# Two transitions between matrix stages of a two-block network: row-panel order, updates in pieces and a pre-norm scale applied after the products

## The reference

```
# block 1 (h is meta + x, 272 rows; the meta rows are dropped at the end)
u = rms_norm(h, norm_mix_pre)
u = conv mixer(u): (u @ w_in) -> a * sigmoid(g) -> causal depthwise conv, 31 taps
                   -> layer_norm -> silu -> @ conv_w_out + b_out
h = h + rms_norm(u, norm_mix_post)                              # first transition
u = (silu(n @ w_gate) * (n @ w_up)) @ w_down,  n = rms_norm(h, norm_ffn_pre)
h = h + rms_norm(u, norm_ffn_post)                              # second transition
# block 2
proj = rms_norm(h, norm_mix_g_2) @ w_in_2      -> b, c, hc, z, gate logits
y    = short conv(b, c, hc) @ w_up_conv, spatial gating(gelu(z)) @ w_up_sgu
h = h + (sig(g1)*y1 + sig(g2)*y2) @ w_out_2                     # third transition
n = rms_norm(h, norm_ffn_g_2); router picks 1 of 4 groups and 2 of its 4 experts
h = h + sum over chosen experts of gate * ((silu(n@wg) * (n@wu)) @ wd)
out = rms_norm(h, norm_final_g_2)
rms_norm(x, g) = x * rsqrt(mean(x*x) + 1e-6) * g
```

## Time and profile before

| | |
|---|---|
| timed runs | 2414.32 us median (2413.07 to 2415.45) |
| profiled execution | 2415.2 us, span 2413.2 us |
| TensorE busy | 2320.2 us (96%) |
| VectorE, ScalarE, GpSimd busy | 1599.2 (66%), 1273.8 (53%), 174.2 us (7%) |
| mean granted clock of TensorE | 0.974 |
| DMA | 510.87 MB, mean 212 GB/s |

### The profile page before, as it was taken

One profiled execution on the slowest core, in us unless ns is written; L12 is line 12 of the kernel. 1 busy time (PEld: TensorE's weight loads), 2 busy tenths in 40 slices (PEclk: granted clock), 3 DMA queues, 4 the chain that ended last, 5 costly groups with the idle time before them and its releaser, 6 DMA issues.

```text
span 2413.2 us, 34884 instructions
## 1 busy us (share of the span) xinstructions
PE 2320.2 (96%) x12133; PEld 1976.1 (82%) x12133; DVE 1599.2 (66%) x1785; ACT 1273.8 (53%) x1243; POOL 174.2 (7%) x67
## 2 busy tenths in 40 slices
PE   9999897999999999997999999999979999999997
PEld 8999686888888878886888888887767777777775
DVE  3999666555555554446576654575568888888887
ACT  4444446555555544445443544443346776766775
POOL 4676000000000000000020000000000000000000
PEclk8999898999999999998999999999979999999998
DMA  7555155666766745555576676654529989899894
GB/s 199 167 156 168 70 194 154 188 187 181 192 191 187 193 159 191 192 192 183 146 202 184 172 192 191 180 177 171 187 79 341 348 315 365 318 347 339 316 365 187
DMA packets 494081, 510.87 MB, mean 212 GB/s; under 512 B 12204, under 2 KB 407108, under 8 KB 475076
## 3 DMA queue, kind: packets, MB, share of 16 engines
q1 hardware_dynamic: 492660, 504.30, 65.6%
q0 software_dynamic: 1104, 5.78, 0.7%
q10 hardware_dynamic: 272, 0.20, 0.0%
HBM read 508.15 MB, written 2.10 MB: 211 GB/s over the span
## 4 chain that ended last, share of the span: by engine, by line
PE 85%; DVE 6%; ACT 4%; DMA 2%; issue 2%; ACTq 0%; DVEq 0%; SPq 0%
PE ps L1785 23%; PE ps L1725 17%; PE ps L1790 12%; PE ps L1918 7%; PE ps L1934 6%; PE ps L1922 4%; ACT whi L522 3%; PE ps L1635 3%; PE ps L1636 2%; PE ps L1658 2%; DVE wlo L926 2%; PE ps L1820 2%; DMA raw<-in_w_exp_up 1%; PE ps L1899 1%; DMA raw<-in_w_exp_gate 1%
## 5 line engine op out<-in xcount | busy, mean ns | idle before, releaser
L926 DVE TENSOR_TENSOR wlo<-raw,whi 128x2048 fp32r<-128x2048 f32 x444 | 1017.3, 2292 | 338.7 <-ACT whi L522 337.2
L522 ACT ACTIVATE whi<-raw 128x2048 fp32r<-128x2048 f32 x476 | 911.6, 1916 | 535.1 <-PE ps L1725 220.1
L1785 PE MATMUL ps<-xT,whi 128*128 128x512 f32 x2688 | 647.6, 392 | 7.3 <-DVE xT L1278 4.2
L1785 PEld LDWEIGHTS ps<-xT,whi 128*128 128x128 f32 x2688 | 494.8, 189 | 103.5 <-issue 4.4
L1790 PEld LDWEIGHTS ps<-xT,wlo 128*128 128x128 f32 x2688 | 347.1, 191 | 15.7 <-DVE wlo L926 1.3
L1790 PE MATMUL ps<-xT,wlo 128*128 128x256 f32 x2688 | 351.6, 283 | 0.9 <-DVE wlo L926 0.9
L1725 PE MATMUL ps<-whi,act 128*128 128x512 f32 x1168 | 282.5, 395 | 3.2 <-ACT act L619 3.2
L1725 PEld LDWEIGHTS ps<-whi,act 128*128 128x128 f32 x1168 | 223.0, 191 | 52.4 <-ACT act L619 3.7
L1918 PE MATMUL ps<-whi,moe_r 128*128 128x512 f32 x1024 | 258.3, 394 | 6.1 <-ACT whi L522 6.1
L694 ACT ACTIVATE wk<-ps 128x256 f32<-128x256 f32 x184 | 68.8, 384 | 353.0 <-PE ps L1790 352.7
L1918 PEld LDWEIGHTS ps<-whi,moe_r 128*128 128x128 f32 x1024 | 191.5, 189 | 49.5 <-ACT whi L522 7.6
(11 more groups left out here) (263 smaller groups left out, 1748.3 us busy)
## 6 DMA issues: line engine op xcount, KB each, us to landing
raw<-in_w_in SPq DMA_DIRECT2D x72, 1024.0 KB, 5.5
raw<-in_w_exp_gate SPq DMA_DIRECT2D x64, 1024.0 KB, 5.4
raw<-in_w_exp_up SPq DMA_DIRECT2D x64, 1024.0 KB, 5.7
raw<-in_w_exp_down SPq DMA_DIRECT2D x64, 1024.0 KB, 5.9
raw<-in_ffn_w_gate SPq DMA_DIRECT2D x44, 1024.0 KB, 5.6
raw<-in_ffn_w_up SPq DMA_DIRECT2D x44, 1024.0 KB, 5.6
raw<-in_ffn_w_down SPq DMA_DIRECT2D x44, 1024.0 KB, 4.8
raw<-in_conv_w_in SPq DMA_DIRECT2D x32, 1024.0 KB, 6.0
```

Of the source, the lines that this page charges most:

```text
L522: fn(whi[:, s % 2, :], raw[:, s % RING, :], ACT.Copy).then_inc(hi_ready, 1)
L926: V.tensor_tensor(wlo[:, s % 2, :], raw[:, s % RING, :], whi[:, s % 2, :], ALU.subtract).then_inc(lo_ready, 1)
L1785: mm(ps[:, bank, :], whi[:, s % 2, at:at + P], xT5[:, k0 + k, :], start=(k == 0), stop=False)
```

## The change

- **Last two row panels** (`last_row_pair` for `last_row_panel`, three stages): both panels' products of token half 0 first, `tok_done` after each of its four pieces; then half 1 piece by piece, with a `tok_done` for each.
- **`post`** (ScalarE, VectorE): waits for each piece by itself; `h` is updated in 512-column pieces, each telling `add_done`. ScalarE's first high half of the next stage comes behind the squares.
- **No scale before the turn**: `pre` is gone at the first two transitions. TensorE turns the unscaled rows of `h` as an ordinary fp32 product with the identity. The squares of `h` (`row_squares`), roots and reciprocals come after the turn. The reciprocals become a 128x256 broadcast: VectorE scales the identity (`rs_d`), TensorE multiplies by `ones` (`scale_rows`), VectorE copies it (`rsB`).
- **The scale is applied later**: in the feed-forward to the gate panel after `joined` (the up panel's scale goes into the post-norm's epsilon, `BIAS2`), in ZV's gelu by per-row scalars, and in CH, BG, U, GT to every panel after `joined` (one product more on VectorE).
- **GpSimd makes the first two low halves** of C and of ZV, once all updates of `h` are done; TensorE waits for `lo_pool` there.
- At the first transition TensorE runs panels 0 and 1 of the feed-forward interleaved with the turns; at the second it turns tiles 8 to 15 between the products of ZV's first two panels.
- At the third transition, the adds wait for single pieces; `pre` stays.

```diff
# GpSimd
+            def lo(n, s, added):
+                pool.wait_ge(add_done, added)
+                pool.wait_ge(hi_ready, n + s + 1)
+                pool.tensor_tensor(wlo[:, s, :], raw[:, s, :], whi[:, s, :], ALU.subtract).then_inc(lo_pool, 1)
+            lo(C, 0, 8)
+            lo(C, 1, 8)
             pool.wait_ge(post_done, 8)
             pool.dma_start(gB[:, :], norm_ffn_post.to_broadcast([P, D])).then_inc(gain_in, 16)
+            lo(ZV, 0, 16)
+            lo(ZV, 1, 16)
...
# ScalarE
             post(0, C)
-            turn(1, V_FPRE, 0)
+            turn(1, V_FPRE, 0, C, {4: 1})          # hi(C, 1) ahead of tile 4
+            row_squares(0, 0)
+            hi(C, 2)
+            row_squares(0, 1)
+            row_roots(0)
...
+            turn(2, V_MIX2, 4, ZV, {8: 1, 12: 2})
+            row_squares(1, 0)
+            row_squares(1, 1)
+            row_roots(1)
...
# VectorE
+                def added(t):
+                    v.wait_ge(root_ready, 2 + 4 * q + t + 1)
+                    own.mark(V.reciprocal(st[:, RS + t:RS + t + 1], st[:, RT + t:RT + t + 1]))
+                    own.wait(v)
+                    v.wait_ge(post_done, 8 * q + NC * (t + 1))
+                    for c in range(NC):
+                        hc = h[:, t, c * BANK:(c + 1) * BANK]
+                        V.scalar_tensor_tensor(out=hc, in0=tmp[:, t, c * BANK:(c + 1) * BANK], scalar=st[:, RS + t:RS + t + 1],
+                                               in1=hc, op0=ALU.mult, op1=ALU.add).then_inc(add_done, 1)
+                for b in range(NC):
+                    gained(b)
+                total(q, 0)
+                gained(NC)
+                gained(NC + 1)
+                added(0)
+                total(q, 1)
+                gained(NC + 2)
+                gained(NC + 3)
+                added(1)
...
+            def joined(f, s, bank, dst, scaled=None):
                 v.wait_ge(feat_half, f + (s + 1))
-                V.tensor_tensor(dst, ps[:, bank, 0:T], t1[:, s % 2, :], ALU.add).then_inc(feat_free, 1)
+                ins = V.tensor_tensor(dst, ps[:, bank, 0:T], t1[:, s % 2, :], ALU.add)
+                if scaled is not None:
+                    own.mark(ins)
+                    own.wait(v)
+                    ins = V.tensor_tensor(dst, dst, rsB[scaled], ALU.mult)
+                ins.then_inc(feat_free, 1)
...
# TensorE
+            def last_row_pair(n, step):
+                for s in (2, 3):
+                    pe.wait_ge(hi_ready, n + (s + 1))
+                    pe.wait_ge(act_hi, step + s + 1)
+                    part(s, 0, whi, 0, range(NC))
+                    pe.wait_ge(act_lo, step + s + 1)
+                    part(s, 1, whi, 0, range(NC))
+                    pe.wait_ge(lo_ready, n + (s + 1 - B))
+                    for c in range(NC):
+                        i = part(s, 0, wlo, 0, (c,))
+                        if s == 3:
+                            i.then_inc(tok_done, 1)
+                for c in range(NC):
+                    for s in (2, 3):
+                        part(s, 0, whi, 1, (c,))
+                        part(s, 1, whi, 1, (c,))
+                        i = part(s, 0, wlo, 1, (c,))
+                        if s == 2 and c == NC - 1:
+                            i.then_inc(mm_done, 1)
+                    i.then_inc(mm_done if c == NC - 1 else tok_done, 1)
...
+            def turn_rows_of(q, i, bank, halves=range(TOK)):
+                for t in halves:
+                    pe.wait_ge(add_done, 8 * q + NC * t + (NC if t == 0 else i // 2 + 1))
+                    for k in range(2):
+                        at = (2 * i + k) * P
+                        ins = mm(ps[:, bank + i % 4, k * T + t * P:k * T + (t + 1) * P], h[:, t, at:at + P], ident[:, :], start=True, stop=True)
+                if 1 in halves:
+                    ins.then_inc(turned, 2)
...
-            turn(1, 0)
+            for i in range(4):
+                turn_rows_of(0, i, 0, (0,))
+            for i in range(4):
+                turn_rows_of(0, i, 0, (1,))
+            pe.wait_ge(feat_free, F_C + 2)
+            pe.wait_ge(hi_ready, C + 1)
+            for i in range(4, KT // 2):
+                pe.wait_ge(xlo_ready, KT + 2 * (i - 3))
+                turn_rows_of(0, i, 0)
+                hi_product(0, 2 * i - 8)
+                hi_product(0, 2 * i - 7)
+            pe.wait_ge(hi_ready, C + 2)
+            for k in range(KT // 2, KT):
+                pe.wait_ge(xlo_ready, KT + k + 1)
+                hi_product(0, k)
+                hi_product(1, k - KT // 2)
...
-            turn(2, 4)
+            pe.wait_ge(add_done, 8 + NC + 1)
+            for i in range(4):
+                turn_rows_of(1, i, 4)
             for b in range(4):
                 open_bank(b)
             for q in range(8):
+                if q == 1:
+                    late_rows(6)
+                    late_rows(7)
...
                 banks(0, whi)
                 banks(1, whi)
+                if q == 0:
+                    late_rows(4)
+                    late_rows(5)
+                if q < 2:
+                    pe.wait_ge(lo_pool, 2 * KT + 2 + q + 1)
+                else:
+                    pe.wait_ge(lo_ready, ZV + q + 1 - B)
                 banks(0, wlo).then_inc(mm_done, 1)
+                if q == 4:
+                    pe.wait_ge(xlo_ready, 3 * KT)
+                    scale_rows(2, 4)
+            pe.wait_ge(rs_copied, 1)
```

More of the change, by code:

```diff
@@ L635, in b_group @@
                 for s in range(4):
-                    if not (last and s == 3):
+                    if not (last and s >= 2):
                         hi(j + B, s + 2)
@@ L678, in pre, with turn @@
                     root(st[:, SS + t:SS + t + 1], st[:, RT + t:RT + t + 1], 1.0 / D, st[:, EPS_AT:EPS_AT + 1])
-            def turn(count, gain, bank):
+            def turn(count, gain, bank, n, panels):
                 for k in range(KT):
+                    if k in panels:
+                        hi(n, panels[k])
                     a.wait_ge(turned, KT * count + k + 1 + (k + 1) % 2)
@@ L700, in _ @@
                     half(g * 4 + F_C, s, 4 + s)
-                    hi(g * 4 + C, s + 2)
+                    if not (first and s == 0):
+                        hi(g * 4 + C, s + 2)
                     if s % 2:
@@ L1143, in _ @@
                         v.wait_ge(hid_ready, g * 2 + (s // 2 + 2))
-                    joined(g * 4 + F_C, s, 4 + s, xs[:, 2 if s % 2 else s // 2, :])
-                    lo(g * 4 + C, s + 2)
+                    joined(g * 4 + F_C, s, 4 + s, xs[:, 2 if s % 2 else s // 2, :], scaled=None if s % 2 else 0)
+                    if not (first and s < 2):
+                        lo(g * 4 + C, s + 2)
                     if s % 2:
@@ L1151, in _ @@
                         V.tensor_tensor(tile_of(tiles, g * 2, s // 2), sg[:, s // 2, :], xs[:, 2, :], ALU.mult).then_inc(hid_ready, 1)
+            c_group(0, first=True)
+            with rounds(v, FT // 2 - 1, (own, 4)) as g:
+                c_group(g + 1)
             def rows(n0, src, step, count):
@@ L1228, in _ @@
                     own.wait(v, 1)
[L1229 removed]
+                    joined(r * 4 + f, s, 4 + s, xs[:, s % 2, :], scaled=1)
                     lo(r * 4 + BG, s + 2)
@@ L1243, in _ @@
             own.wait(v)
-            with rounds(v, CT // 4, (own, 4)) as r:
+            with rounds(v, CT // 4, (own, 8)) as r:
                 for s in range(4):
@@ L1792, in feature_panel, with feature_stage @@
                 return i
-            def feature_stage(n0, f0, count, arrival=None):
-                peeled = 1 if arrival else 0
-                for s in range(4 * peeled):
-                    feature_panel(n0, s, f0 + s + 1, 4 + s, arrival=None if s else arrival).then_inc(mm_done, 1)
-                with pe.Fori(peeled, (count) // 4) as r:
+            def feature_stage(n0, f0, count, first=0):
+                for s in range(first, first and 4):
+                    feature_panel(n0, s, f0 + s + 1, 4 + s).then_inc(mm_done, 1)
+                    if s == first:
+                        scale_rows(1, 0)
+                with pe.Fori(1 if first else 0, (count) // 4) as r:
                     j = r * 4
```

203 lines of the change are left out of this document (117 added, 86 removed).

## The result

| | before | changed |
|---|---|---|
| timed runs | 2414.32 us median (2411.15 to 2417.36, 9 runs) | 2407.83 us median (2405.1 to 2413.27, 9 runs) |
| ratio | | 0.9974, 95% interval 0.9964 to 0.9984 |
| profiled execution | 2415.2 us, span 2413.2 | 2408.69 us, span 2406.9 |
| VectorE, ScalarE, GpSimd busy | 1599.2, 1273.8, 174.2 us | 1636.6, 1216.3, 190.4 us |
| mean granted clock | 0.974 | 0.979 |

The changed kernel is 6.5 us faster, 0.26%. In a second comparison, with both kernels timed beside two others, the ratio was 0.9968 (0.9956 to 0.998).

The account below looks back on a forecast made before the run. TensorE was busy nearly all the span, so only its waits and slow stretches could be won. 6.7 + 4.5 + 1.1 - 3.5 - 0.5 = 8.3 us off 2415.2 gave 2406.9 profiled, 2406 for the median; range 2399 to 2413.

Parts of the forecast that it names:

- Edit 1: Last two row panels run as a pair in three stages: TensorE stalls 0.6 us for VectorE's low half at each.
- Edits 2 and 3: First transition: updates by pieces, unscaled rows turned, panels 0 and 1 interleaved; gain 7.2 less 0.5 = 6.7 us.
- X: Forecast end of the last row product in the changed kernel: T + 0.6 us, the stall of the paired panels included.
- T: The end of TensorE's last row product ahead of a transition, from which times there are counted.
- Edit 4: Second transition: TensorE idles until X + 4.15, the clock is taken as down, then unscaled rows are turned; gain 4.5 us.
- rival A: No lock behind ZV and a clock kept through the second transition's gap: 14 us gained, 2400 us; chance 0.2.
- Edit 5: Added scale products: 3.5 us lost at the fourth CH panel behind ZV, 0.5 at the first gate panel.
- the lock: VectorE's instructions with two SBUF inputs and GpSimd's share a port pair exclusively, so they wait in turn; 3.5 us behind ZV.
- Edit 6: Third transition, updates by pieces only: turns start at T + 6.5 instead of T + 7.6; gain 1.1 us.
- B: The lock costs 5.5 us and the clock falls in the first transition: 1.3 us gained, 2413 us; chance 0.2.
- C: Fp32 identity products neither hold nor raise the clock: first transition 9.4 us later, second 4.4; 2420 us; chance 0.06.

Follow-up runs that it names:

- e6: Kernel before with only the paired last row panels, updates by pieces and the changed third transition; scale still ahead of the transposes: 2411.94 us, one run.
- e3: Changed kernel with GpSimd's low halves no longer waiting for the updates of h: 2415.5 us, one run.
- e7: Changed kernel with the first transition's two low halves made by VectorE instead of GpSimd: 2409.82 us, one run.
- e5: Changed kernel with fp32 products that lead nowhere added in the second transition's gap and ahead of the fourth CH panel: 2410.14 us, one run.
- e4: Changed kernel without the scale products behind the joins of CH, BG, U and GT: 2404.0 us, one run.
- e2: Changed kernel with the rows of h turned by TensorE transposes instead of fp32 products with the identity: 2402.21 us, one run.
- e8: Changed kernel with transposes for feature tiles 8 to 15 alone, identity products kept for tiles 0 to 7: 2408.09 us, one run.

## Why the prediction was right

The forecast was 2406.9 for the profiled execution (2408.69 came) and 2406 for the median (2407.83). By its steps:

- *Edit 1, stall of 0.6 us at each stage.* From row to row about 0.8, 0.8 and 0.7, of which 0.42 stands in the record as the wait for `wlo`. The forecast booked it in the gains of the three transitions, so I take it off the columns below. In the DN column, +1.1, the other 0.3 is the first panel at a low clock.
- *Edits 2 and 3, first transition.* Updates were to end at X + 1.65 and X + 5.8; with X = T here they end at T + 1.7 and T + 5.8. The third panel was to start at X + 22.05 and starts at T + 21.8. Predicted 7.2 less 0.5 = 6.7, measured 7.7 less 0.8 = 6.9. The forecast's 401.15 for the third panel before stands in the earlier trace rows as 401.26, and its 0.6 us for an update is 0.7 (2.74 / 4). e6 confirms that the pieces are the small part, e3 that GpSimd must stand behind the updates, e7 that its help is worth 0.25.
- *Edit 4, second transition.* Idle 3.84 (4.15 predicted), 5.47 for the products (5.7), CH at T + 57.9 (58.5). The forecast set its 1186.9 against 1191.4, but the row is at 1191.64, so by its own terms it had 4.7. Predicted 4.5, measured 5.9 less 0.8 = 5.1. The clock fell as the forecast took it to; e5 prices the fall at 1.6 us, against 2.2 in rival A.
- *Edit 5, the lock.* Predicted 3.5 + 0.5, measured by e4 3.5 + 0.5, with another 0.5 in that column that e4 has too. The make-up differed, and the equal sums are luck in part. The forecast took 3.5 us of pure wait and left the clock out. The wait was 2.85, a wait of 0.91 of the kernel before went, and the clock fell in the wait: the sixteen narrow products behind it took 3.58 us instead of 2.08. e2, e3 and e8 have the same wait (2.85 to 2.87), but the clock held and the narrow products took 2.17 to 2.18; their column is 1.4 us lower. So about 2.1 us are the lock's and 1.4 the clock's. The Trainium skill's rule of an exclusive lock for the whole instruction (SBUF — State Buffer, section SBUF: two separate sides) fits the alternation, and e3 shows a larger case of it than the forecast used: two instructions of 0.7 us each waited for one of 4.9.
- *Edit 6, third transition.* The restart wait is 5.79 (5.9 predicted), -1.7 less the stall of 0.7: 1.0 against 1.1.
- *Not foreseen:* 0.6 to 0.7 us at the up panels, where the clock was down for longer behind the gap of 4.28 us (4.18 before), and the scatter of 5 us of the conv stage's clock, as large as the gain.
- *The sum.* The foreseen terms measured 6.9 + 5.1 + 1.0 - 3.5 - 0.5 = 9.0 us, against 8.3. Behind ZV 0.5 more was lost, at the up panels 0.7, ahead of the first T and in the DN stage 0.3 each, and behind the last product 1.5; the last column gave 0.6 back. That makes the 6.3 us of the spans. The parts ahead of the first T, in the last column and behind the last product differ by 5.0, 1.8 and 1.1 us between the two profiles of the changed kernel, so the total says less for the forecast than the terms by stage do.

Of the rivals, A failed on the lock and on the clock. B's fall of the clock in the first transition did not come, and the lock with the fall behind it cost 3.5 us, not 5.5. The terms that C names for its first transition add up to about X + 29, not X + 31.5, so its 2420 should have been some 2 us less. C is refuted by the first transition, where the clock stayed at 1.00 under the products with the identity, and by e5, where nothing but fp32 products ran for nearly 8 us and it stayed there too.

## What to carry to other kernels

A per-row scale that stands between an update and the transposes of its rows can go behind the next products, and that, with the next products started between the turns, is what shortens the transition, and not cutting the update in pieces; but count what the added products share a port with in the first microseconds of their stage. Beside GpSimd, put VectorE's two-input instructions where nobody waits for them. Here gaps of 3.84 and 4.28 us cost TensorE 1.6 and 2.0 us more in clock; spare products won that back, and nothing in the gaps ahead of the router and the experts, where another wait stood right behind.

## What was not expected of the hardware

- Four updates of 512 columns took 11.25 us beside two GpSimd instructions of 4.9 us, 2.74 without them. VectorE's splits, with an operand in PSUM, took 0.40 us each beside such instructions, as without.
- An fp32 128x128 product with the identity costs 0.24 us at the full clock (3.84 / 16); a transpose 0.13 there (1.03 / 8) and 0.19 at a mostly low clock (2.99 / 16). The products held the clock at 1.00 through idle pieces of 1.73 and 0.93 us; with transposes, and 1.02 us more of idle time between them, it fell. Behind gaps of 3.84 and 3.85 us it was back 3.9 us after the first product and 7.6 after the first transpose.
- Fp32 products with few columns (the router's 20) let the clock fall though they follow each other without idle time: 3.75 us for the first sixteen at the full clock, 6.92 for the next.
- One kernel's clock came back 5 us earlier or later behind the same gap, from one execution to the next.
